# A mixer and expert kernel on one core: eight places in the program order changed around the first expert blocks

## The reference, cut to what matters

```
probs = softmax(h1 @ w_router)                    # 16 experts in 4 groups
eidx  = two best experts of the best group        # per row
gate  = probs[eidx] / sum(probs[eidx])
rows are sorted by expert, each expert's rows padded to blocks of 128
for each block of 128 rows xb with expert e:
    hid = silu(xb @ w1[e]) * (xb @ w3[e])         # 1024 -> 512
    y   = hid @ w2[e]                             # 512 -> 1024
out = LayerNorm(alpha * h1 + sum over the two experts of gate * y)
```

## Time and profile before

| | |
|---|---|
| median of three runs | 1367.25 us (1366.76 to 1369.74) |
| the profiled execution | 1365.61 us |
| its span (first to last instruction) | 1363.6 us |
| PE busy | 1317.3 us, 97% of the span |
| DVE busy | 958.1 us, 70% |
| ACT and POOL busy | 512.3 and 520.1 us, 38% each |
| DMA | 243.58 MB, mean 179 GB/s |

### The profile page before, as it was taken

How to read it: one execution, slowest core, us unless ns; L and a number is a source line. 1 busy time by engine, 2 the same in 40 slices (tenths; PEclk the granted TensorE clock), 3 DMA queues, 4 the chain that set the end, 5 groups by cost and what they waited for, 6 DMA issues and landing times.

```text
span 1363.6 us, 20422 instructions
## 1 busy us (share of the span) xinstructions
PE 1317.3 (97%) x6386; PEld 1101.3 (81%) x6387; DVE 958.1 (70%) x1353; ACT 512.3 (38%) x570; POOL 520.1 (38%) x544
## 2 busy tenths in 40 slices
PE   4999999999999999999999999999999999999994
PEld 4988888888888888787788888888888888888883
DVE  7667667697759685788588875765675677776573
ACT  2433233322343233324345543442533445434340
POOL 1001110121101110021466665656566666666564
PEclk9999999999999999998999999999999999999997
DMA  9525444464455345624977774564554545666411
GB/s 265 161 78 164 147 123 170 155 193 118 154 183 158 108 139 174 212 95 147 350 264 263 262 253 162 172 237 147 181 195 184 189 176 210 239 232 230 138 54 63
DMA packets 156522, 243.58 MB, mean 179 GB/s; under 512 B 18944, under 2 KB 84992, under 8 KB 156480
## 3 DMA queue, kind: packets, MB, share of 16 engines
q1 hardware_dynamic: 118624, 154.15, 34.7%
q0 software_dynamic: 28928, 71.74, 14.9%
q10 hardware_dynamic: 8928, 17.13, 3.7%
HBM read 211.97 MB, written 64.62 MB: 203 GB/s over the span
## 4 chain that ended last, share of the span: by engine, by line
PE 93%; DVE 2%; issue 1%; DMA 1%; POOL 1%; POOLq 0%; ACT 0%; SPq 0%; DVEq 0%; ACTq 0%
PE acc L507 28%; PE acc L509 28%; PE acc L508 28%; PE tp L540 4%; PE logits L579 1%; PE aux L781 1%; DMA xg<-h_scratch,gat_now 1%; PE logits L727 1%; DMA b_in<-in_ln_in_b 0%; PE aux L509 0%; PE aux L508 0%; PE aux L507 0%; PE aux L619 0%; DVE hres L1099 0%; DVE xt_lo L1430 0%
## 5 line engine op out<-in xcount | busy, mean ns | idle before, releaser
L507 PE MATMUL acc<-ring_hi 128*128 128x512 f32 (+1 forms) x800 | 309.3, 387 | 4.4 <-DVE ring_lo L1126 4.4
L509 PE MATMUL acc<-ring_hi,ring_lo 128*128 128x512 f32 (+1 forms) x800 | 306.0, 382 | 0.0
L508 PE MATMUL acc<-ring_lo,ring_hi 128*128 128x512 f32 (+1 forms) x800 | 305.8, 382 | 0.0
L507 PE MATMUL acc<-ring_hi,xt_hi 128*128 128x512 f32 x640 | 253.4, 396 | 4.6 <-DVE xt_lo L1430 4.6
L509 PE MATMUL acc<-ring_hi,xt_lo 128*128 128x512 f32 x640 | 250.2, 391 | 0.0
L508 PE MATMUL acc<-ring_lo,xt_hi 128*128 128x512 f32 x640 | 250.1, 391 | 0.0
L1643 POOL TENSOR_TENSOR small<-small 128x1 f32<-128x1 f32 x32 | 46.9, 1467 | 364.5 <-DVE small L1093 364.5
L507 PEld LDWEIGHTS acc<-ring_hi 128*128 128x128 f32 x800 | 151.8, 190 | 32.3 <-DVE ring_lo L1126 4.8
L509 PEld LDWEIGHTS acc<-ring_hi,ring_lo 128*128 128x128 f32 x800 | 151.7, 190 | 29.1
L508 PEld LDWEIGHTS acc<-ring_lo,ring_hi 128*128 128x128 f32 x800 | 151.8, 190 | 27.6
L832 ACT CAST ring_hi<-stage_x 128x2048 fp32r<-128x2048 f32 x64 | 119.5, 1917 | 76.6 <-PE acc L509 76.1
(11 more groups left out here) (251 smaller groups left out, 1872.7 us busy)
## 6 DMA issues: line engine op xcount, KB each, us to landing
stage_x<-in_exp_w SPq DMA_DIRECT2D x64, 1024.0 KB, 6.6
stage<-in_w_in SPq DMA_DIRECT2D x64, 512.0 KB, 5.4
stage<-in_exp_w SPq DMA_DIRECT2D x32, 1024.0 KB, 6.5
stage<-in_w_out SPq DMA_DIRECT2D x32, 512.0 KB, 5.2
h_scratch<-hres POOLq DMA_DIRECT2D x16, 512.0 KB, 3.0
sum_scratch<-hres ACTq DMA_DIRECT2D x16, 512.0 KB, 2.9
hrow<-in_x POOLq DMA_DIRECT2D x12, 512.0 KB, 4.7
h_scratch<-hrow POOLq DMA_DIRECT2D x12, 512.0 KB, 3.0
```

Source lines behind the costliest of these rows:

```text
L507: nc.tensor.matmul(dst, w_hi, x_hi, start=start, stop=False)
L508: nc.tensor.matmul(dst, w_hi, x_lo, start=False, stop=False)
L509: return nc.tensor.matmul(dst, w_lo, x_hi, start=False, stop=stop)
```

## The change

Eight edits, on four engines:

1. SP: the wait for gather 1 (`s_gat` at 32) stood ahead of all loads of expert 1; now it stands ahead of unit 2 of expert 1, so units 0 and 1 can be loaded as soon as their staging slots are free.
2. PE: `ranks(2)` in the last chunk is moved from behind unit 8 to behind the first tile of unit 9.
3. PE: `h1_last(0)` no longer waits for all residuals of the last chunk, and `h1_last(1)` waits only for the second residual of the last half.
4. PE: `x_tile(1)` is moved from behind `down(0)` to between its two halves.
5. DVE: `hid_lo(0)` is moved ahead of the three operations that write `by_col`.
6. DVE: `x_lo(1)` is moved from behind the tables to the middle of them, ahead of `tb_a`.
7. POOL: `index_rows(1)`, `index_rows(2)` and `gather_rows(2)` are moved ahead of `index_sums(0)` and `gather_sums(0)`.
8. `down` takes an argument for edit 4.

```diff
@@ sync @@
-            sp.wait_ge(s_gat, 32)
             for ex in range(1, NE):
                 for j in range(EU):
+                    if ex == 1 and j == 2:
+                        sp.wait_ge(s_gat, 32)
                     sp.wait_ge(s_elo[j // 2], (ex - 1) * 2 + j % 2 + 1)
                     load_expert(ex, j)
@@ tensor, chunk @@
                         if j == 8 and t == 1:
                             pool_map(c, 3)
+                        if last and j == 9 and t == 0:
+                            ranks(c - 1)
...
-                    if last and j == 8:
-                        ranks(c - 1)
@@ tensor, h1_last @@
                 pe.wait_ge(s_h1, LAST * TPC + t + 1)
-                if t < 2:
-                    pe.wait_ge(s_res, NCH * 2 * TPC)
-                else:
+                if t == 1:
+                    pe.wait_ge(s_res, NCH * 2 * TPC - TPC + 2)
+                elif t >= 2:
                     pe.wait_ge(s_h1tc, (LAST * TPC + t - 1) * 2)
@@ tensor, down @@
-            def down(e_of):
+            def down(e_of, rows_of=None):
                 for h in range(2):
+                    if rows_of is not None and h == 1:
+                        x_tile(rows_of)
                     pe.wait_ge(s_elo[2], e_of * 2 + h + 1)
...
-            down(0)
-            x_tile(1)
+            down(0, 1)
@@ vector @@
             tt(whole[:], lists[:].rearrange("p k c -> p (k c)"), aux[:], ALU.add)
+            hid_lo(0)
             V.tensor_tensor(by_col[:, :, 0], whole[:, 0:COLS], whole[:, COLS:], ALU.min)
             V.tensor_copy(by_col[:, :, 1], whole[:, 0:COLS])
             V.tensor_copy(by_col[:, :, 2], whole[:, COLS:]).then_inc(s_plist, 1)
-            hid_lo(0)
             first_expert_lo(EU - 1)
...
             ch.link(V.tensor_tensor_scan(end[:], row_1[:], nblk[:], 0.0, ALU.mult, ALU.add))
+
+            x_lo(1)
...
-            x_lo(1)
             dve.wait_ge(s_elo[2], 2)
             turn(1, True)
@@ gpsimd @@
             index_rows(0)
+            index_rows(1)
+            index_rows(2)
+            gather_rows(2)
             index_sums(0)
             pool.wait_ge(s_szero, 1)
             gather_sums(0)
-            index_rows(1)
-            index_rows(2)
-            gather_rows(2)
```

## The result

| | before | after |
|---|---|---|
| median (22 runs each, taken side by side) | 1367.22 us | 1371.09 us |
| lowest to highest | 1365.28 to 1373.26 | 1367.56 to 1374.91 |
| ratio, with 95% interval | | 1.0019 [1.001, 1.0028] |
| profiled execution, its span | 1365.61, 1363.6 us | 1369.79, 1367.8 us |
| mean granted clock over the span | 0.992 | 0.989 |

The forecast was 1365.0 us with a range up to 1367.4. The kernel came out slower, and outside the range. By the medians alone the ratio would be 1.0028. The 22 times of the kernel before fall into two groups, 15 of up to 1368.2 us (median 1366.4) and 7 of 1369.6 us and more (1370.1), and the experiments come back to this.

The account below looks back on a forecast made before the run. PE, busy 93% of the span, was taken as the bound. Block 2 came 3.7 or 2.6 us earlier; with one slow stretch (+1.7) in all, -2.0 to -2.6, taken as -2.25 from 1367.25: 1365.0 us, range 1362.8 to 1367.4.

Parts of the forecast that it names:

- Edits 2 and 3, -2.1: PE, up to `hid_tile(0)`: the mask wait of 1.2 us and residual wait of 0.9 go; 633.35 instead of 635.46.
- The part on the clock: One slow stretch moves from `down(0)` to block 2 (-2.0), or the one in `down(0)` stays and none is added (-2.6).
- Edit 5, -0.3: PE ahead of `down(0)`: the wait for `ht_lo` shrinks by 0.3 us, not 1.7; cast and subtraction remain.
- Edits 4 and 6: Block 1 starts at 642.25, 5.3 us earlier, or 4.1 if the clock falls; `x_tile(1)` waits 0.45 on gather 1.
- The tables: On DVE, ready at 645.45 (0.35 us earlier) or 646.6 (0.8 later); last `nblocks` write within 1 us of 645.8.
- ACT: Block 1: three table reads, 2.3 us in all, hold `silu(1)` until 649.65; block 2 at 659.4, 3.7 us earlier.
- Edit 7, "up to a landing of 6.5 us it costs nothing": Ahead of block 2: gather 2, issued at 649.75 with landing 5.5 us, costs nothing; a landing of 8.2 costs 1.7.
- a sign of being wrong: Ahead of block 2: the prediction is wrong if gather 2 lands later than 6.5 us after its issue.
- The slow stretch at block 2, +1.7: Behind 4.7 us of PE waiting ahead of block 2, a stretch of low clock was expected, costing 1.7 us.
- After block 2: A microsecond won on PE is kept to the end as long as the blocks behind stay bound by PE.
- Rival D: Block 2: the sums' gather, issued later, holds up gather 3; up to 1.5 us lost, 1366.5 us; chance 0.10.
- Rival E: Late gather 1 delays the tables on DVE, `silu(1)` and block 2; +2.1 or +3.8, 1369.4 to 1371 us; chance 0.07.

Follow-up runs that it names:

- ln2_behind: The full change with ACT's two loads of the norm's rows issued only behind gather 2's landing; ratio 1.0016 to the kernel before.
- ln2_zero: The full change with ACT's two norm loads behind gather 2's landing and POOL's zeroing of `srow` ahead of gather 1; ratio 1.001 to the kernel before.
- blocks14567: The kernel before with edits 1, 4, 5, 6 and 7 alone, mixer and router as they were; ratio 1.0018 to the kernel before.
- only2: The kernel before with edit 2 alone (`ranks(2)` later on PE); ratio 0.9995 to the kernel before.
- only3: The kernel before with edit 3 alone (residual waits of `h1_last` cut); ratio 0.9997 to the kernel before.
- sums_first: Edits 1 to 6 with POOL's order of before, `srow` zeroed ahead of gather 1, ACT's two norm loads behind gather 2's landing; ratio 1.0025 to the kernel before.

## Why the prediction was wrong, point by point

- **Edits 2 and 3, -2.1.** The waits went, as forecast, and the router started 2.8 us earlier. This step failed: "`hid_tile(0)` at 633.35". It came at 637.53, since the router's slow stretch grew from 3.4 to 13.6 us. The part on the clock priced one stretch in `down(0)` and one at block 2 and never looked at 612 to 629 us, where the trace of before already had 0.90; a longer stretch there was put at nothing without a reason. The loss here, 4.9 us in the trace, is nearly three times the 1.7 us at which the prediction priced a stretch. In the times it is less, since part of the executions of before seem to have it too: 7 of the 22 beside this kernel lie in the upper group, and in the sessions of the experiments 71 of 128.
- **Edit 5, -0.3.** Right for PE: the wait for `ht_lo` is 1.47 (forecast 1.4). Its price on DVE was overlooked: DVE now waits 0.61 us for `ht_hi`, and `by_col` slides under POOL's zeroing, 0.7 more.
- **Edits 4 and 6.** The wait on gather 1 was 0.41 (forecast 0.45), the `xt_lo` wait gone, block 1 9.28 us after `hid_tile(0)` (forecast 642.25 - 633.35 = 8.9), `down(0)` at full clock. The tables: forecast 12.1 from `hid_tile(0)`, measured 12.69, the 0.6 being the `by_col` cast. By the clock of the span they are 4.6 us later and not "within 1 us", most of it the router's.
- **ACT.** Right: `act_a` of block 1 was released by ACT's own issue, 16.23 us after `hid_tile(0)`, forecast 649.65 - 633.35 = 16.3.
- **Edit 7, "up to a landing of 6.5 us it costs nothing".** This step failed, and all three of its sizes erred one way. The issue was 1.1 us later than forecast (17.47 against 16.4), of which 0.6 the tables and 0.3 a longer gap on POOL. The landing was 7.3 us. The prediction had priced a late landing ("at 8.2 it costs 1.7") and named one over 6.5 as a sign of being wrong, but the sum went by the median of the rows, 5.5, though the trace of before had this very transfer: issued at 651.64 and waited for until 659.87, 8.2 us. It also had a likely reason, ACT's load at 647.21: of the DMA time from 652 to 655 us that queue had 50.4%, SP's 29.9%. Block 2 came at 28.22 from `hid_tile(0)` and not at 26.05. Ln2_behind bears the step's arithmetic out: with a landing of 4.3 it comes at 25.28, 0.8 before the forecast, and there ACT, without the two loads ahead, starts `silu(1)` 0.9 sooner (15.37 against 16.23).
- **The slow stretch at block 2, +1.7.** It came, but ahead of block 2 and not in it: `x_tile(2)` and `hid_tile(1)` take 1.97 and 1.06 us instead of 1.09 and 0.63, 1.3 more, and the rest of the stretch lay under waits. From block 2 to `x_tile(3)` it is 11.0 us before and after. That it lay ahead of block 2 is this trace's: in the nine kernels with edit 5 in which it lay or reached behind block 2's start (all but ln2_behind and ln2_zero) those 11.0 us were 12.6 to 14.1. There the forecast of +1.7 or more behind block 2 came true. The kernels had up to 10.2 us of slow clock behind `hid_tile(0)`.
- **After block 2.** The forecast had the microsecond "kept to the end as long as the blocks behind stay bound by PE". They didn't stay so. The wait for `ht_lo` in block 2 (1.5 us) is new, but it stands in the trace of the changed kernel alone: in the eleven other traces with edit 5 PE doesn't wait for it, and behind `x_tile(3)` nine of them take 17.7 to 18.0 us to `x_tile(4)`, as before (17.7), where the changed kernel took 19.5. So this term may be one execution's. DVE runs `hid_lo(1)` behind all of the first block's norm. Before, it ended at 674.67, 0.2 us ahead of the matmuls that need it, and this slack was on no row that I had read. Of the 1.3 us by which DVE stood longer ahead of it (2.86 against 1.59, both put down to issue) I know no cause.
- **Rival D** came true in blocks14567, ln2_zero and ln2_behind (1.2, 3.7 and 4.1 us waited for gather 3). It was priced at 1.5 at most, with a chance of 0.10 (in the last two the other waits ahead of it are gone and ACT's loads lie beside the sums' gather, and so it is larger). In the changed kernel itself gather 3 was issued 29.85 us after `hid_tile(0)`, 3.5 later than before, and PE did not wait for it only because block 2 was late itself: with the 7.5 us of blocks14567 it landed at some 37.4 (an estimate), `x_tile(3)` came at 39.22, and with block 2 at the forecast 26.05 it would have come at 37.1. **Rival E**, on the losing side, didn't happen: gather 1 landed in time. The loss came by another road.

In sum, for the one trace, from `hid_tile(0)` to `x_tile(4)` the forecast was -1.6 at block 2 and +1.7 for the stretch behind it, +0.1. Measured were +0.6 at block 2, the stretch included, and +1.8 behind it, of which 1.5 for `ht_lo`: +2.35. Ahead of `hid_tile(0)` the forecast was -2.1 and the trace shows +2.1. In the measured times (medians +3.9, ratio +2.6) the block part seems the larger: blocks14567 alone has the ratio of the whole change. Which part of that +2.6 is gather 2, the slow clock at block 2 or the waits behind it differs from trace to trace, and stays open.

## What to carry to other kernels

When an edit makes an engine earlier, price the transfer that the engine will next wait for by that transfer's own row, issue to first use, and not by a median over its kind. Then go one stage further down and read how much slack the next two or three hand-overs have. Here gather 2 was already waited for and `ht_lo` had 0.2 us, so 2.9 us won at block 1 turned into a wait at the next. Gather 3 had more, some 4.8 us by an estimate (12.25 us from its issue to its use before, less the 7.5 that it took in blocks14567), and even that was used up where its issue moved by 7 or 8.

Before adding up waits of a microsecond, look at the list of all executions with their mean clock. If it falls into two groups, the choice between them can be worth more than the waits (3.4 us here), and a single trace shows only one. Check a wait that a trace shows in a second trace before you build on it: the 1.5 us for `ht_lo` stood in one of twelve.

## What the runs showed of the hardware

- Around the end of the router a slow stretch of 3.4 or 13.6 us came (6.8 in one trace of eighteen), without any recorded gap on PE in it. The short one began behind the last router product, in block 0's first matmuls (621.2 us in the trace of before). The long one began within the router's products (614.2 in the changed kernel) and ended in block 0's matmuls too. By the mean clocks the length was the one or the other from execution to execution of the same kernel (only2 and only3, 6 to 6 each), and with edits 2 and 3 together it was the long one in nine traces of ten.
- Slow stretches moved more than they went: with `hid_lo(0)` early the one in `down(0)` vanished in each of the twelve traces with that edit, and each of these had one or more later on, ahead of or in blocks 1 to 3.
- A cast of 128x256 on DVE took 1.08 us instead of 0.32 beside a memset on POOL, and POOL's issue of a gather took 2.2 to 2.6 us instead of 1.05 when it started during one of DVE's subtractions of 128x2048.
- The same 0.53 MB gather took 4.3 or 4.5 us to land with ACT's loads out of its way and little of SP's beside it, 6.4 to 7.4 with ACT's two loads issued ahead in the kernels with edit 6, and 8.2 to 8.8 in the kernel before and in sums_first. How far the loads are the cause is not shown.
